# Expert weights of a fused diffusion step: from the seventh expert on, 4 MB loads with 32 KB rows instead of 2 MB loads with 16 KB rows

## The reference

```
def expert_choice_ffn(h, p):                 # n = 128 context or 256 latent tokens, D = 2048
    aff = softmax(xs @ p['w_router'])        # 16 experts, capacity 16 + 32 = 48 slots
    g, idx = lax.top_k(aff.T, cap)
    xe = xs[idx]
    a = einsum('ecd,edf->ecf', xe, p['w_exp_gate'])    # 2048 x 1024 per expert
    u = einsum('ecd,edf->ecf', xe, p['w_exp_up'])      # 2048 x 1024
    ye = einsum('ecf,efd->ecd', silu(a) * u, p['w_exp_down']) * g   # 1024 x 2048
    out = zeros((n, D)).at[idx].add(ye)
```

## Time and profile before

| | |
|---|---|
| timed runs | 2276.83 us median of 3 (2276.82 to 2277.99) |
| profiled execution | span 2276.0 us from the first to the last instruction, no other time is given for it |
| TensorE busy | 2164.1 us, 95% of the span, mean granted clock 0.998 |
| VectorE, ScalarE busy | 1074.7 us, 377.8 us |
| DMA | 647.84 MB, mean 285 GB/s; hardware queue of SP and ACT 68.6% of 16 engines |
| loads of 2048 KB from w_gate_up into the ring | 96, median 15.7 us from issue to landing |
| chain that ended last | TensorE 73%, DMA 19% (w_gate_up 14%) |

### The profile page before, as it was taken

One profiled execution on the slowest core, in us unless ns is written; L12 is line 12 of the kernel. 1 busy time (PEld: TensorE's weight loads), 2 busy tenths in 40 slices (PEclk: granted clock), 3 DMA queues, 4 the chain that ended last, 5 costly groups with the idle time before them and its releaser, 6 DMA issues.

```text
span 2276.0 us, 26579 instructions
## 1 busy us (share of the span) xinstructions
PE 2164.1 (95%) x10773; PEld 1366.1 (60%) x10773; DVE 1074.7 (47%) x1704; ACT 377.8 (17%) x953; POOL 138.1 (6%) x144
## 2 busy tenths in 40 slices
PE   6999999999999999999999999999998988889997
PEld 2389974467899999999987753333332222223223
DVE  6188998776778678676663430111001110102114
ACT  3011110012444432101001221011100000000002
POOL 0001100013111110000000000100000000000000
PEclk9999999999999999999999999999999999999999
DMA  9955554343432434445464389999999999999997
GB/s 385 427 217 198 198 210 158 153 156 117 185 149 111 185 129 168 185 157 199 162 259 153 127 308 421 420 428 426 428 427 428 427 422 428 427 428 423 427 425 302
DMA packets 54878, 647.84 MB, mean 285 GB/s; under 512 B 6214, under 2 KB 6760, under 8 KB 10216
## 3 DMA queue, kind: packets, MB, share of 16 engines
q1 hardware_dynamic: 52568, 637.66, 68.6%
q10 hardware_dynamic: 2192, 8.52, 0.9%
HBM read 642.47 MB, written 3.69 MB: 284 GB/s over the span
## 4 chain that ended last, share of the span: by engine, by line
PE 73%; DMA 19%; DVE 3%; DVEq 2%; issue 1%; ACT 1%; ACTq 0%; POOL 0%; SPq 0%; POOLq 0%
PE PS L943 27%; DMA ring<-in_w_gate_up 14%; PE PS L1632 10%; PE PS L1675 7%; PE PS L801 5%; PE PS L1426 4%; PE PS L1120 3%; PE PS L1410 2%; PE PS L1593 2%; DMA ring<-in_w_ada 2%; PE PS L1107 2%; DMA ring<-in_w_down 1%; PE PS L1716 1%; PE PS L790 1%; DMA ring<-in_w_down_last 1%
## 5 line engine op out<-in xcount | busy, mean ns | idle before, releaser
L1632 PE MATMUL PS<-ring,RF 128*48 128x512 f32 x1424 | 328.7, 596 | 46.1 <-DMA ring<-in_w_gate_up 44.4
L2537 DVE SCALAR_TENSOR_TENSOR GX<-ring,SM,GX 128x512 f32<-128x512 f32 x450 | 329.5, 770 | 17.4 <-issue 1.3
L1632 PEld LDWEIGHTS PS<-ring,RF 128*48 128x48 f32 x1424 | 89.6, 123 | 270.2 <-issue 186.7
L943 PE MATMUL PS<-RB,ring 128*128 128x192 f32 x1376 | 233.3, 327 | 0.8 <-ACT RE L1892 0.8
L943 PEld LDWEIGHTS PS<-RB,ring 128*128 128x128 f32 x1376 | 224.9, 190 | 6.9 <-ACT RE L1892 2.0
L3432 DVE TENSOR_TENSOR RB<-RB,PS 128x512 f32<-128x512 f32 x84 | 55.8, 686 | 348.5 <-PE PS L1593 348.4
L3437 DVE TENSOR_TENSOR GX<-RF,PS 48x512 f32<-48x512 f32 x32 | 22.1, 690 | 294.7 <-ACT RF L2193 262.8
L1675 PE MATMUL PS<-ring,RF 128*48 128x512 f32 x688 | 152.0, 594 | 3.9 <-DMA ring<-in_w_down 3.7
L943 PE MATMUL PS<-RE,ring 128*128 128x192 f32 x768 | 130.1, 326 | 0.0
L801 PE MATMUL PS<-ring,RB 128*128 128x512 f32 x288 | 126.9, 593 | 0.0
L943 PEld LDWEIGHTS PS<-RE,ring 128*128 128x128 f32 x768 | 124.9, 190 | 0.1
(11 more groups left out here) (473 smaller groups left out, 2988.3 us busy)
## 6 DMA issues: line engine op xcount, KB each, us to landing
ring<-in_w_gate_up SPq DMA_DIRECT2D x96, 2048.0 KB, 15.7
ring<-in_w_ada SPq DMA_DIRECT2D x48, 2048.0 KB, 9.2
ring<-in_w_down SPq DMA_DIRECT2D x40, 2048.0 KB, 15.8
ring<-in_w_in SPq DMA_DIRECT2D x38, 2048.0 KB, 8.4
ring<-in_w_gate_up SPq DMA_DIRECT2D x26, 1024.0 KB, 11.2
ring<-in_w_attn_o SPq DMA_DIRECT2D x8, 2048.0 KB, 8.0
ring<-in_w_out SPq DMA_DIRECT2D x8, 2048.0 KB, 8.2
GX<-in_w_gate_up SPq DMA_DIRECT2D x8, 2048.0 KB, 17.8
```

The lines of the kernel that those rows point to most:

```text
L943: last = mm(bank(b, TH), w(k), x(k), start=start and k == 0, stop=k == kn - 1, skip_group_check=not start)
L1632: last = mm(bank(n, p0=64 * u, p1=64 * u + SLOTS), xeT[:, 0, kk, :] if first else x_cur[:, kk, :], part_of(home_of(at, 2 * i + u), k * FF ...
L2537: last = stt(out=acc[c], in0=w, scalar=cond[:, kk, c:c + 1], in1=acc[c], op0=ALU.mult, op1=ALU.add)
```

## The change

From expert 6 on, two neighbouring units are one quad: 4 MB, 128 rows of 32 KB. The host writes a second copy of the layout for experts 6 to 15 (`w_gate_up_late`, `w_down_late`), in which each partition's row holds both units. There are three homes of 4 MB: the two halves of the ring, and a third that reaches from GX into RE (the two tensors are allocated as one, GXE; the part in RE covers the inputs of experts 0 to 5). A quad is waited for and released as a whole: SP waits for the use of its second unit. Exceptions: units 0 and 1 of expert 6 and units 6 and 7 of expert 15 travel as 2 MB halves of a quad (16 KB rows, 32 KB apart in HBM). The 16 quarters of 1 MB stay, now with 12 homes instead of 8. `g2_rows`, `ones2` and `f_g` move within RE.

```diff
+        GXE = sb("GXE", 2048 + 3840 + 2 * MT * D)
+        GX, RE = GXE[:, 0:5888], GXE[:, 5888:5888 + 2 * MT * D]
...
+        quads = [view(ring_t, 0, 8 * FF), view(ring_t, 8 * FF, 8 * FF), view(GXE, 1792, 8 * FF)]
+        unit_r = quads[2][:, 4 * FF:8 * FF]
+        down_homes = [quads[(j // 4 + 2) % 3][:, j % 4 * 2 * FF:(j % 4 + 1) * 2 * FF] for j in range(12)]
...
-        LISTED = 10
+        LISTED = 6
...
+            def unit_free(e, u):
+                if u < 7:
+                    sp.wait_ge(piece_used, e * RELEASES + 2 * (u + 1))
+                elif u < 8:
+                    sp.wait_ge(gu_done, e * 2 + 2)
+                elif u < 11:
+                    sp.wait_ge(piece_used, e * RELEASES + 14 + 2 * (u - 7))
+                else:
+                    sp.wait_ge(down_done, e * 2 + 2)
+
+            def load_quad(e, r):
+                sp.dma_start(quads[r % 3], gate_up_quad(e, r) if r < 4 else down_quad(e, r - 4)).then_inc(quad_in[r % 3], 16)
+
+            def sixth_expert():
+                e = LISTED
+                sp.wait_ge(xe_st, LISTED - 1)
+                sp.dma_start(unit_r, gate_up_quad(e, 0)[:, 0:4 * FF]).then_inc(unit_in[0], 16)
+                piece_free(*last_of(3))
+                sp.dma_start(pairs[:, 1, :], gate_up_quad(e, 0)[:, 4 * FF:8 * FF]).then_inc(unit_in[1], 16)
+                piece_free(*last_of(7))
+                load_quad(e, 1)
+                piece_free(*last_of(18))
+                unit_free(e, 0)
+                load_quad(e, 2)
+                piece_free(*last_of(1))
+                unit_free(e, 1)
+                load_quad(e, 3)
+                unit_free(e, 3)
+                load_quad(e, 4)
+                unit_free(e, 5)
+                load_quad(e, 5)
+
             def expert(e):
-                for q in range(0, PIECES, 2):
-                    if q < 6:
-                        sp.wait_ge(piece_used, e * RELEASES + (q - 5))
-                    elif q == 6:
-                        sp.wait_ge(down_done, e * 2)
-                    elif q < 22:
-                        sp.wait_ge(piece_used, e * RELEASES + (q - 6))
-                    else:
-                        sp.wait_ge(gu_done, e * 2 + 2)
-                    load_pair(e, q)
+                for r in range(6):
+                    unit_free(*((e - 1, 2 * r + 7) if r < 3 else (e, 2 * r - 5)))
+                    load_quad(e, r)
...
+                for r in range(4):
+                    unit_free(*((e - 1, 2 * r + 7) if r < 3 else (e, 1)))
+                    load_quad(e, r)
+                for r, free in enumerate(((e, 3), (e, 5), (e, 7))):
+                    unit_free(*free)
+                    sp.dma_start(quads[(r + 1) % 3], gate_up_quad(e + 1, r)).then_inc(quad_in[(r + 1) % 3], 16)
+                unit_free(e + 1, 0)
+                unit_free(e + 1, 1)
+                for h in range(2):
+                    sp.dma_start(pairs[:, 2 + h, :], gate_up_quad(e + 1, 3)[:, h * 4 * FF:(h + 1) * 4 * FF])\
+                        .then_inc(unit_in[2 + h], 16)
...
+            def quad_landing(e, q):
+                if e == LISTED and q < 4:
+                    if q % 2 == 0:
+                        pe.wait_ge(unit_in[q // 2], unit_landed(q // 2))
+                elif e == NE - 1 and q >= 12:
+                    if q % 2 == 0:
+                        pe.wait_ge(unit_in[2 + (q - 12) // 2], unit_landed(2 + (q - 12) // 2))
+                elif q % 4 == 0:
+                    n = quad_no(e, q // 4)
+                    pe.wait_ge(quad_in[n % 3], quad_landed(n))
```

More of the change, by code:

```diff
@@ L408, in build @@
             AHEAD + FORMS[1:] + LATENT + RING[:2] + FORMS[:1] + RING[2:] + \
-            CONTEXT + SPLIT + AHEAD + LATENT + FORMS[1:] + (RING + FORMS) * 12 + RING * 6
-        LISTED = 10
+            CONTEXT + SPLIT + AHEAD + LATENT + FORMS[1:] + (RING + FORMS) * 8
+        LISTED = 6
         def home_of(e, q):
-            return HOMES[e * PIECES + q] if e < LISTED else q % 8
+            return HOMES[e * PIECES + q]
         def sem_of(home):
@@ L446, in part_of, with last_of, listed_on, quad_landed @@
             return split_a[:, at:at + NC_] if at < 3 * NC_ else split_b
+        def last_of(home):
+            return divmod(max(g for g in range(LISTED * PIECES) if home_of(*divmod(g, PIECES)) == home), PIECES)
+        QUAD_SEM, UNIT_SEM, QUARTER_SEM = (0, 4, 8), (9, 10, 11, 1), (2, 3, 5, 6, 7, 9, 10, 0, 4, 8, 11, 1)
+        quad_in, unit_in, quarter_in = ([piece_in[n] for n in ns] for ns in (QUAD_SEM, UNIT_SEM, QUARTER_SEM))
+        def listed_on(n):
+            return 16 * sum(sem_of(home_of(*divmod(g, PIECES))) == n for g in range(LISTED * PIECES)
+                            if g < 3 * PIECES or g % 2 == 0)
+        def quad_landed(n):
+            return listed_on(QUAD_SEM[n % 3]) + 16 * (n // 3 + (0 if n % 3 == 0 else 1))
+        def unit_landed(j):
+            return listed_on(UNIT_SEM[j]) + 16
+        def quarter_landed(q):
+            n = QUARTER_SEM[quarter_slot(q)]
+            last = quad_no(NE - 1, 2)
+            quads_on = max(quad_landed(i) for i in range(last - 2, last + 1) if QUAD_SEM[i % 3] == n) if n in QUAD_SEM else \
+                listed_on(n)
+            return quads_on + (16 if n in UNIT_SEM else 0) + 16 * (q // 12 + 1)
+        def quarter_slot(q):
+            return q if q < 12 else (0, 1, 4, 5)[q - 12]
+        def quad_no(e, r):
+            return 6 * (e - LISTED) + r - (2 if e == NE - 1 else 0)
         def behind(e, q):
@@ new lines, in last_two @@
+                unit_free(e + 1, 0)
[3 more added lines that the diff above has]
+                        .then_inc(unit_in[2 + h], 16)
+                base = e * RELEASES
+                for q in range(16):
+                    if q < 4:
+                        sp.wait_ge(piece_used, base + 14 + 8)
+                    elif q < 8:
+                        sp.wait_ge(piece_used, base + 14 + 12)
+                    elif q < 10:
+                        sp.wait_ge(piece_used, base + 28)
+                    elif q < 12:
@@ L710, in last_two @@
                         sp.wait_ge(gu_done, 2 * e + 4)
                     elif q % 2 == 0:
-                        sp.wait_ge(piece_used, base + 28 + ((q - 40) // 2 + 1))
+                        sp.wait_ge(piece_used, base + 28 + (quarter_slot(q) // 2 + 1))
                     else:
-                        sp.wait_ge(down_done, 2 * e + ((q - 40) // 2 + 1))
-                    sp.dma_start(pieces[:, q % 8, :], down_quarter(q % 4 // 2, (q - 32) // 4, q % 2))\
-                        .then_inc(piece_in[q % 8], 16)
+                        sp.wait_ge(down_done, 2 * e + (quarter_slot(q) // 2 + 1))
@@ L718, in _ @@
+                    sp.dma_start(down_homes[quarter_slot(q)], down_quarter(q % 4 // 2, q // 4, q % 2))\
+                        .then_inc(quarter_in[quarter_slot(q)], 16)
             for c in range(4):
@@ L728, in _ @@
                 listed_expert(e)
-            with sp.Fori(LISTED, NE - 2) as e:
+            sixth_expert()
+            with sp.Fori(LISTED + 1, NE - 2) as e:
                 expert(e)
@@ L1594, in scatter, with late_part, weights_at, expert @@
                        ye[0:64 + SLOTS, 2 * i + u, :], start=True, stop=True).then_inc(e_sc, 1)
-            def expert(e, pair=None, turn=None, at=LISTED, rest=None, gates=False):
-                first = at == 0
+            def quad_landing(e, q):
[8 more added lines that the diff above has]
+                    pe.wait_ge(quad_in[n % 3], quad_landed(n))
+            def late_part(e, q, at):
+                if e == LISTED and q < 4:
+                    unit_at_, within = (unit_r if q < 2 else pairs[:, 1, :]), q % 2
+                elif e == NE - 1 and q >= 12:
+                    unit_at_, within = pairs[:, 2 + (q - 12) // 2, :], q % 2
+                else:
+                    unit_at_, within = quads[quad_no(e, q // 4) % 3], q % 4
+                return unit_at_[:, within * 2 * FF + at:within * 2 * FF + at + NC_]
+            def weights_at(e, q, at):
+                return late_part(e, q, at) if e >= LISTED else part_of(home_of(e, q), at)
+            def expert(e, pair=None, turn=None, rest=None, gates=False):
+                first = e == 0
                 def beside(t):
@@ L1606, in landing @@
                 def landing(q):
[L1607 to L1610, removed]
+                    if e >= LISTED:
+                        quad_landing(e, q)
+                    elif e < 3 or q % 2 == 0:
+                        home = home_of(e, q)
+                        pe.wait_ge(piece_sem(home), steps_of(home) * loads_of(e, q) + before_pieces(home))
                 if not first:
@@ L1681, in expert @@
                         last.then_inc(piece_used, 1)
[L1683 to L1688, removed]
+            expert(0)
+            expert(1, turn=0)
+            expert(2, pair=0)
+            expert(3, turn=1, rest=0)
+            expert(4, pair=1)
```

(22 more changed lines are left out.)

55 lines of the change are left out of this document (15 added, 40 removed).

## The result

| | before | changed |
|---|---|---|
| median of 8 runs | 2276.82 us (2274.31 to 2277.99) | 2282.91 us (2281.77 to 2283.49) |
| ratio, 95% interval | | 1.0029 (1.0021 to 1.0038) |
| span of the profiled execution | 2276.0 us | 2281.0 us |

The median is 6.1 us above before, 10.0 us above the forecast of 2272.9 and outside its range.

A forecast was written before the change was run, and what follows sets the result against it. The weight stream, landing at a fixed step, was taken as the bound from before expert 6 to the end of expert 15's gate/up. Fewer packets gave -3.9 us, all else 0: 2276.83 - 3.9 = 2272.9 us, range 2270.9 to 2277.1.

The forecast's parts named there:

- Fewer packets: Weight stream, experts 6 to 15: 144 fewer packets a quad at 8.0 ns, 54 quads, 3.9 us less.
- Rows at a longer pitch: Weight loads: engines read rows 32 KB apart in HBM without loss, priced at 0.
- The prediction's 566 us: Cost over the quads if loads ran at the skill's 207 GB/s for a 512 KiB pitch; not expected.
- Coarser homes: Experts' loop: homes freed only when both units are used cause no stall, priced at 0.
- the 8.0 us to spare: Even experts, between units 7 and 8: release comes at t + 21.4, the stream is busy until t + 29.4.
- The change over, in expert 6: Switch from units to quads: the stream ahead covers the waits for homes, priced at 0.
- The end: Experts 14 and 15 to the quarters: TensorE comes 1.3 us later, but the 13th quarter's landing covers it, 0.
- The rivals: Rows cut at 16 KB (0.17), a code packet spared (0.10), long rows slower (0.07), homes stall (0.06).
- The stall rival: Five even experts, 6 to 14: each overruns its margin by 2 us, 2282.9 us in all; chance 0.06.
- The prediction's last sentence: A wrong prediction would show as unevenly spaced quads, a home released late, or a later stream start in expert 6.

The follow-up runs named there:

- e2_before_late_release: The kernel before, with only its loads of units 6 and 7 of expert 15 held back until unit 5 is used: 2283.78 us, ratio 1.0032.
- e5_release_one_unit_late: As e1_release_right, but in experts 7 to 13 each quad is loaded one used unit later: 2283.14 us, ratio 1.0030.
- e1_release_right: The changed kernel with the wait ahead of units 6 and 7 of expert 15 set to unit 1's use: 2272.54 us, ratio 0.9983.
- e8_changed_with_longer_fill: The changed kernel, late release kept, with 17 products of constants on TensorE between units 5 and 6 of expert 15: 2283.98 us, ratio 1.0035.
- e7: The changed kernel, late release kept, with 11 products of constants on TensorE between units 5 and 6 of expert 15: 2284.66 us, ratio 1.0038.

## Why the prediction was wrong

- **Fewer packets, 54 x 0.072 = 3.9 us: right.** Packets per MB halved, quads land 9.72 us apart (9.71 was worked out). With the wait mended the kernel is 3.4 us faster (2272.54 against 2275.96; the interval of the ratio allows 1.8 to 5.9), and all of it goes again, 3.6 us, when the rows are cut to 16 KB. The price of 8.0 ns a packet, fitted to two windows, held for a size of packet that the trace of before did not have.
- **Rows at a longer pitch, 0: right.** Two loads of 16 KB rows 32 KB apart took 9.79 us, as units whose rows follow one another did. No run here shows a pitch near the 512 KiB of the Trainium skill's rule (DMA: Bandwidth & Descriptors, Latency and other measured facts). The prediction's 566 us can't be drawn from that rule either: its 207 GB/s are for copies between two HBM tensors, where it calls 214 the full rate, and not for loads into SBUF.
- **Coarser homes, 0: the time right, the margin too wide.** Landings in the loop stayed 9.72 us apart. But the 8.0 us to spare leave out the start of a load: a 2 MB load of 4.9 us took 7.15 us from issue to landing in an empty queue, 2.3 us more (2.7 more in e2_before_late_release). That leaves 5.7 at best, and the late landings of e5_release_one_unit_late, with 3.2 to 7.3 us ahead, say that even this is not sure. How much later a release may come stays open.
- **The change over, in expert 6: right**, no late landing there.
- **The end: the step that failed.** The prediction takes the landings of units 6 and 7 of expert 15 from the times of before ("landed 2214.88"), calls the stream ahead of the quarters full, and prices the end at 0. It has no term for the release ahead of these two units. I took `unit_free(e + 1, 1)` by its name, as the use of unit 1 of expert 15. By its number it waits for unit 5, until 2208.0 us. The queue ran empty, and unit 6 landed 14.35 us behind the last quad instead of 4.9. At the last landing of gate/up that makes 4.2 us won and 9.45 lost: unit 7, 4.9 us behind unit 6, came at 2220.14 instead of 2214.88, 5.3 us late, and the span grew by 5.0. The rest of the step holds once the wait is mended: in e1_release_right TensorE reached the 13th quarter at 2243.9, where 2248.7 less the 3.9 us, 2244.8, had been worked out.
- **The clock**, which I did not price, fell after waits that quads make longer (0.96 over 1680 to 1760 us). No run shows a cost of it: with the same clock there e1_release_right lands its quads 9.72 us apart, and with the end's wait filled e8_changed_with_longer_fill is no faster.

The rivals missed it too. The stall rival's 2282.9 us is the measured time, but that is luck: it put 2 us on each of five even experts, where landings stayed even, and took each wait to mean what it says. The prediction's last sentence did name the kind of fault, a home released late, but no place for it. The cause is shown from three sides: mended, the loss is gone; put into the old kernel, the wait costs 7.8 us; at a middle dose it costs a part.

The version that beats both kernels is the changed one with that one wait mended, 2272.54 us, ratio 0.9983 (0.9974 to 0.9992).

## What to carry to other kernels

Where a change rewrites waits on counting semaphores, put numbers into every one of them and find the instruction that reaches each number, above all where an epilogue reorders the work that the count assumes: a wait that is too high is correct, free of races, and silent. In a stream that is bound by its rate, price a change in load size as packets saved times the cost of one, taken from windows with different packet sizes. The mark of a queue that ran empty is one load in the chain with a much shorter issue to landing than its neighbours.

## What the runs showed of the hardware

- A row of 32 KB goes as one packet, and its rate lies on the line through those of the 8 and 16 KB rows (8.0 ns a packet): 422, 428 and 431 GB/s.
- A load of 2 MB into an empty queue took 7.15 us from issue to landing in the changed kernel and 7.63 in e2_before_late_release, 2.3 to 2.7 us more than the 4.9 between landings; in a full queue it doesn't show, since quads landed 9.72 us apart there.
- After a wait of 2.7 us between dense matmuls the granted clock of TensorE still fell (e7: 32 matmuls in 8.71 us instead of 7.07); after 7.6 us filled with products of constants (e8) it stayed at 1.00. The length of the wait alone doesn't decide it: in e1_release_right 32 matmuls behind a wait of 2.54 us took 7.07 us (at 1742.00), and 8.77 behind one of 1.96 us (at 1937.84).
